# Narrow key ranges in a dilated attention, and another order of the opening transfers, in an f32 kernel of four joined layers

## The reference

```python
DILATION_GROUPS = ((128, 1), (512, 4), (2048, 16))     # (window, dilation)
# 8 query heads, 2 key/value heads, head dimension 128, 512 tokens
# causal dilated window: query t sees keys t, t-d, t-2d, ..., t-window
for g, (window, dilation) in enumerate(DILATION_GROUPS):
    o, l = dilated_window_attention(q[:, :, g], k[:, :, g], v[:, :, g], window, dilation)
...
wts = softmax(stack(lses))                              # over the three groups
o = sum(wts[..., None] * stack(outs))
```

## Time and profile before

| | us |
|---|---|
| Median of 3 runs (lowest, highest) | 3950.6 (3949.82, 3952.23) |
| The profiled execution, its own time | 3940.59 |
| Its span | 3938.6 |
| PE busy | 3680.1 (93% of the span) |
| DVE busy | 2036.6 (52%) |
| ACT busy | 798.5 (20%) |
| POOL busy | 1004.8 (26%) |
| Mean granted PE clock | 0.971 |
| DMA | 295.50 MB, mean 75 GB/s |

### The profile page before, as it was taken

The page is one execution under the profiler, slowest core; times in us unless marked ns, Lnnn a source line. Parts: engine busy times, 40 slices in busy tenths (PEclk is TensorE's granted clock), DMA queues, the critical chain, the costliest instruction groups (busy, mean ns, idle before and its releaser), DMA issues. The chain is left out here.

```text
span 3938.6 us, 37971 instructions
## 1 busy us (share of the span) xinstructions
PE 3680.1 (93%) x14476; PEld 2535.4 (64%) x14476; DVE 2036.6 (52%) x3522; ACT 798.5 (20%) x1606; POOL 1004.8 (26%) x964
## 2 busy tenths in 40 slices
PE   5999987999999999997899999999999998889999
PEld 3577334555555546633688884688886544778887
DVE  5820567676675530147664465755534224765543
ACT  2101455110010110154311113211111111421110
POOL 0100540322323100052334430234430000034443
PEclk9999998999999999998999999999999998999999
DMA  5422100133331111210122222222222210012222
GB/s 222 149 81 72 33 26 19 64 104 120 109 121 59 70 52 55 71 49 29 33 74 87 86 86 73 75 75 86 87 95 80 71 54 32 1 44 89 92 86 86
DMA packets 52100, 295.50 MB, mean 75 GB/s; under 512 B 5424, under 2 KB 5552, under 8 KB 25552
## 3 DMA queue, kind: packets, MB, share of 16 engines
q1 hardware_dynamic: 37808, 244.32, 18.1%
q10 hardware_dynamic: 9504, 31.98, 2.4%
q0 software_dynamic: 4608, 16.78, 1.3%
HBM read 290.57 MB, written 2.49 MB: 74 GB/s over the span
## 5 line engine op out<-in xcount | busy, mean ns | idle before, releaser
L2179 POOL TENSOR_TENSOR scratch<-ring 128x512 f32<-128x512 f32 (+1 forms) x148 | 187.3, 1265 | 1950.9 <-PE psum L575 1200.7
L575 PE MATMUL psum<-big,scratch 128*128 128x256 f32 (+1 forms) x2240 | 605.6, 426 | 0.0
L550 PE MATMUL psum<-H,ring 128*128 128x512 f32 x1184 | 560.5, 608 | 23.8 <-ACT H L1144 11.5
L575 PEld LDWEIGHTS psum<-big,scratch 128*128 128x128 f32 x2240 | 425.6, 190 | 163.7
L575 PE MATMUL psum<-H,scratch 128*128 128x256 f32 (+1 forms) x1856 | 435.7, 389 | 4.5 <-ACT cb L1074 3.2
L575 PE MATMUL psum<-big,ring 128*128 128x256 f32 (+1 forms) x1520 | 403.9, 418 | 13.7 <-DVE big L1719 4.9
L575 PEld LDWEIGHTS psum<-H,scratch 128*128 128x128 f32 x1856 | 350.6, 190 | 74.7 <-ACT cb L1074 8.7
L575 PE MATMUL psum<-H,ring 128*128 128x256 f32 (+1 forms) x1408 | 375.1, 411 | 9.4 <-ACT H L1144 4.2
L550 PEld LDWEIGHTS psum<-H,ring 128*128 128x128 f32 x1184 | 229.5, 195 | 237.1 <-issue 222.8
L575 PEld LDWEIGHTS psum<-big,ring 128*128 128x128 f32 x1520 | 287.7, 190 | 115.9 <-DVE big L1719 6.5
L575 PEld LDWEIGHTS psum<-H,ring 128*128 128x128 f32 x1408 | 272.3, 194 | 84.5 <-issue 9.3
(11 more groups left out here) (307 smaller groups left out, 4775.8 us busy)
## 6 DMA issues: line engine op xcount, KB each, us to landing
ring<-in_wall SPq DMA_DIRECT2D x202, 1024.0 KB, 4.9
big<-in_wada SPq DMA_DIRECT2D x48, 512.0 KB, 3.5
big<-in_wada POOLq DMA_DIRECT2D x32, 512.0 KB, 3.9
H<-negd ACTq DMA_DIRECT2D x16, 768.0 KB, 5.1
big<-in_wada ACTq DMA_DIRECT2D x4, 2048.0 KB, 28.3
scratch<-in_rpb ACTq DMA_DIRECT2D x16, 448.0 KB, 3.7
X<-in_xin SPq DMA_DIRECT2D x1, 3072.0 KB, 14.3
out<-X SPq DMA_DIRECT2D x1, 2048.0 KB, 7.2
```

The lines of the kernel that those rows point to most:

```text
L550: mm = pe.matmul(bank(b), lhsT, rhs_x(k0 + k), start=first, stop=last)
L575: mm = pe.matmul(fast_bank(st, q, b), lhsT, rhs(k), start=start and k == 0, stop=k == kt - 1, skip_group_check=True)
L2179: pool.tensor_tensor(s1, a21, a22, ALU.add).then_inc(combo_own, 1)
```

## The change

In the dilated attention, the 128 queries of a unit are cut into four blocks a of 32 (tokens 128a to 128a+127). A block needs at most the 256 keys from 128*max(a-1, 0) on, and only those are now computed. Scores of group 0 become four products of 32 queries with 256 keys, each writing its 32 partitions of PSUM; the values of group 0 become eight products (two key tiles for each of four blocks) of 32 queries, which accumulate into 32 partitions each. Masks, scores, exponentials, transposes and copies have 512 columns in place of 768; the mask tensor has 1280 columns in place of 2304. The units, the lists of the engines and their waits stay.

In the opening, X is sent in four parts, each with a semaphore of its own, after the constants and after the first group of modulation weights has landed; the ring slots wait for the third group. ACT waits for `cb` before it issues the modulation weights, and its squares wait for the parts of X one by one. Names of the unused branches are removed.

```diff
-NMASK2 = DIL * SEQ + 2 * P
+NMASK2 = DIL * 2 * P + 2 * P
...
-        x_in = sem("x_in")
+        x_in = [sem(f"x_in{g}") for g in range(4)]
...
+        ATTN = [(h, p) for h in range(QH2) for p in range(DIL)]
+
+        def near(a):
+            return max(a - 1, 0)
...
             sp.dma_start(cb[:], cvec.to_broadcast([P, 2 * D])).then_inc(cb_in, 16)
-            sp.dma_start(X_[:], xin).then_inc(x_in, 16)
...
             sp.dma_start(pos_s[0:ROPE2, :], pos.to_broadcast([ROPE2, SEQ])).then_inc(consts_in, 16)
-            for g in range(2):
-                sp.wait_ge(first_in[g], 16)
+            sp.wait_ge(first_in[0], 16)
+            for g in range(4):
+                at = slice(2 * g * TOK, 2 * (g + 1) * TOK)
+                sp.dma_start(X_[:, at], xin[:, at]).then_inc(x_in[g], 16)
+            sp.wait_ge(first_in[2], 16)
...
-                        pe.matmul(psum[:, s:s + 512], Q2[:, h, q * P:(q + 1) * P], K2[:, kv, :], start=True, stop=True)
...
+                    for a in range(4):
+                        pe.matmul(psum[32 * a:32 * a + 32, s:s + 256], Q2[:, h, q * P + 32 * a:q * P + 32 * a + 32],
+                                  K2[:, kv, near(a) * P:near(a) * P + 256], start=True, stop=True)
...
-                    for c, _ in key_tiles(u):
-                        mm = pe.transpose(psum[:, 2048 + c:2048 + c + P], Ssb[u % 2][:, c:c + P], ident)
+                    for c in range(4):
+                        mm = pe.transpose(psum[:, 2048 + c * P:2048 + (c + 1) * P], Ssb[u % 2][:, c * P:(c + 1) * P], ident)
...
-                    for i, (c, vals) in enumerate(kt):
-                        mm = pe.matmul(bank(6 + u % 2, n), PTs[u % 2][:, c:c + P], vals,
-                                       start=(i == 0), stop=(i == len(kt) - 1))
+                    for half in range(2):
+                        for a in range(4):
+                            pe.matmul(psum[32 * a:32 * a + 32, b * 512:b * 512 + P],
+                                      PTs[u % 2][:, half * P + 32 * a:half * P + 32 * a + 32],
+                                      V2[:, 0, near(a) + half, kv:kv + P], start=half == 0, stop=False, skip_group_check=True)
+                    for g in (1, 2):
+                        mm = pe.matmul(bank(b, P), PTs[u % 2][:, (1 + g) * P:(2 + g) * P], V2[:, g, q, kv:kv + P],
+                                       start=False, stop=g == 2, skip_group_check=True)
...
             def squares():
-                act.wait_ge(x_in, 16)
                 for k in range(DT):
+                    act.wait_ge(x_in[k // 2], 16)
                     act.activation(H[:, k, :], X[:, k, :], ACT.Square).then_inc(sq_done, 1)
...
-                    act.activation(Ssb[c][:, a:768], Ssb[c][:, a:768], ACT.Exp, bias=small[:, 194 + c:195 + c],
+                    act.activation(Ssb[c][:, 0:512], Ssb[c][:, 0:512], ACT.Exp, bias=small[:, 194 + c:195 + c],
...
-                    act.activation(PTs[u % 2][:, a:768], psum[:, 2048 + a:2048 + 768], ACT.Copy).then_inc(aPTs, 1)
+                    act.activation(PTs[u % 2][:, 0:512], bank(4), ACT.Copy).then_inc(aPTs, 1)
...
+            act.wait_ge(cb_in, 16)
             for g in range(4):
                 act.dma_start(B_[:, g * 4 * D:(g + 1) * 4 * D].rearrange("p (t k) -> p t k", k=D),
                               wada[4 * g:4 * g + 4].rearrange("t p k -> p t k")).then_inc(first_in[g], 16)
-            act.wait_ge(cb_in, 16)
...
-                        own(dve.scalar_tensor_tensor(x[:, 0:512], psum[:, s:s + 512], g, M2[:, q * 512:(q + 1) * 512],
-                                                     ALU.mult, ALU.add))
+                    own(dve.scalar_tensor_tensor(x[:, 0:256], psum[:, s:s + 256], g, M2[:, q * 256:(q + 1) * 256],
+                                                 ALU.mult, ALU.add))
...
-                    step(dve.tensor_reduce(small[:, 192 + c:193 + c], x[:, a:768], AX_X, ALU.max))
+                    step(dve.tensor_reduce(small[:, 192 + c:193 + c], x[:, 0:512], AX_X, ALU.max))
```

More of the change, by code:

```diff
@@ L778, in mlstm, with dilated_attention @@
                 turn(NH - 1)
-            def attention(which):
-                units = attn_units(which)
-                u0 = sum(UNITS[:which])
+            def dilated_attention():
                 def scores(u):
-                    h, q = units[u]
-                    s = (u % 2) * 1024
+                    h, q = ATTN[u]
+                    kv, s = h // (QH2 // KVH2), (u % 2) * 512
                     if u >= 2:
[L788 to L796, removed]
-                        pe.matmul(psum[:, s:s + 512], Q2[:, h, q * P:(q + 1) * P], K2[:, kv, :], start=True, stop=True)
-                        for g in (1, 2):
-                            mm = pe.matmul(psum[:, s + 384 + g * P:s + 512 + g * P], Q2[:, g * 8 + h, q * P:(q + 1) * P],
-                                           K2[:, 2 * g + kv, q * P:(q + 1) * P], start=True, stop=True)
-                    mm.then_inc(aS, 1)
[L803 to L811, removed]
@@ L830, in values @@
                     mm.then_inc(aO, 1)
                 scores(0)
-                for u in range(len(units)):
-                    if u + 1 < len(units):
+                for u in range(len(ATTN)):
+                    if u + 1 < len(ATTN):
                         scores(u + 1)
@@ L838, in attention @@
                         values(u - 1)
-                values(len(units) - 1)
+                values(len(ATTN) - 1)
             def na_attention(l):
@@ L1021, in _ @@
                 pe.wait_ge(acc_free[p], w.unit // 2)
-            attention(2)
-            pe.wait_ge(aY, sum(UNITS))
+            dilated_attention()
+            pe.wait_ge(aY, len(ATTN))
             turn_y([lambda t, i=i: Y2[:, t - CT, i * P:(i + 1) * P] for i in range(DT)], False)
@@ L1931, in na_attention, with dilated_attention @@
                         between[u]()
[L1933 to L1936, removed]
+            def dilated_attention():
                 def scores(u):
[L1940 to L1945, removed]
+                    h, q = ATTN[u]
+                    s, c = (u % 2) * 512, u % 2
+                    dve.wait_ge(aS, u + 1)
@@ L1946, in scores @@
                     if u >= 2:
-                        dve.wait_ge(aPT, u0 + u - 1)
+                        dve.wait_ge(aPT, u - 1)
                     x = Ssb[c]
[L1949 to L1955, removed]
-                        own(dve.scalar_tensor_tensor(x[:, 0:512], psum[:, s:s + 512], g, M2[:, q * 512:(q + 1) * 512],
-                                                     ALU.mult, ALU.add))
[L1958 to L1965, removed]
@@ new lines, in scores @@
+                    g = small[:, 344 + h * 4 + q:345 + h * 4 + q]
+                    own(dve.scalar_tensor_tensor(x[:, 0:256], psum[:, s:s + 256], g, M2[:, q * 256:(q + 1) * 256],
+                                                 ALU.mult, ALU.add))
+                    for i in (1, 2):
+                        a = 344 + (i * 8 + h) * 4 + q
+                        c0 = 128 + i * P
+                        ins = dve.scalar_tensor_tensor(x[:, c0:c0 + P], psum[:, s + c0:s + c0 + P], small[:, a:a + 1],
+                                                       M2[:, 1024 + (i - 1) * P:1024 + i * P], ALU.mult, ALU.add)
+                        if i == 1:
+                            own(ins)
@@ L1976, in finish @@
                 def finish(u):
-                    h, q = units[u]
+                    h, q = ATTN[u]
                     c = u % 2
-                    dve.wait_ge(aP, u0 + u + 1)
+                    dve.wait_ge(aP, u + 1)
                     r = small[:, 500 + c:501 + c]
                     step(dve.reciprocal(r, small[:, 496 + u % 4:497 + u % 4]))
[L1982 to L1986, removed]
+                    dve.wait_ge(aO, u + 1)
+                    dve.tensor_scalar(Y2[:, q, h * P:(h + 1) * P], bank(6 + c, P), r, None, ALU.mult).then_inc(aY, 1)
+                for u in range(len(ATTN)):
                     scores(u)
@@ L1989, in attention @@
                         finish(u - 2)
-                for u in (len(units) - 2, len(units) - 1):
+                for u in (len(ATTN) - 2, len(ATTN) - 1):
                     finish(u)
@@ L2233, in _ @@
             mix_weights(SW0)
-            pool.wait_ge(aO, sum(UNITS))
+            pool.wait_ge(aO, len(ATTN))
             mix_weights(YB)
@@ L2279, in _constants @@
     j = np.arange(P)[:, None]
-    s = np.arange(SEQ)[None]
+    key = P * np.maximum(j // 32 - 1, 0) + np.arange(2 * P)[None]
     for q in range(DIL):
-        dist = DIL * j + q - s
-        mask[:, q * SEQ:(q + 1) * SEQ] = np.where((dist >= 0) & (dist <= P), 0.0, NEG)
+        dist = DIL * j + q - key
+        mask[:, q * 2 * P:(q + 1) * 2 * P] = np.where((dist >= 0) & (dist <= P), 0.0, NEG)
     dist = j - np.arange(P)[None]
-    mask[:, 2048:2176] = np.where(dist >= 0, 0.0, NEG)
-    mask[:, 2176:2304] = np.where((dist >= 0) & (dist % 4 == 0), 0.0, NEG)
```

(2 more changed lines are left out.)

46 lines of the change are left out of this document (20 added, 26 removed).

## The result

The changed kernel takes 3914.3 us (median of 3 runs, 3910.5 to 3916.3) against 3950.6: ratio 0.9906, 95% interval 0.9883 to 0.9928, so 28 to 46 us less. In a second measurement (4 runs, beside 12 of the kernel before at 3948.9) it took 3917.1: ratio 0.9917 [0.9904, 0.9931], 32 us less. Forecast was 3918, with 32.2 less.

The account below looks back on a forecast made before the run. A closed chain over two units was taken to bound the dilated attention, TensorE close behind, and VectorE's gapless chain the opening. Attention 23.5 + opening 8.7 = 32.2 us less: 3950.6 - 32.2 = 3918, range 3907 to 3936.

Parts of the forecast that it names:

- The narrow passes overlap four ways: Dilated attention: narrow products in four column groups run together, 0.43 us for scores, 0.44 for values; forecast's own case, chance 0.52.
- The rival of pairs: Dilated attention: narrow passes overlap only two ways, TensorE 3.68 us per unit, 9 + 8.7 us less, 3933; chance 0.17.
- that of dispatch: Dilated attention: short passes start 0.07 us apart, 16 value passes take 1.1, 3.6 per unit, 3931; chance 0.12.
- in series: Dilated attention: narrow passes run one after another, 1.72 us for scores, 1.76 for values, kernel slower at 3988; chance 0.07.
- The price of changing shape: TensorE in dilated attention: going to narrow form costs 0.11 us, coming back 0.19, each twice per unit.
- The chain: Dilated attention: closed chain through TensorE, VectorE and ScalarE over two units goes from 7.93 to 6.45 us.
- the mis-sized term: Dilated attention: the cost of going narrow and back, put at 0.11 + 0.19 us in both scores and values.
- The stage: Dilated attention as a whole: 32 units, each 0.74 us shorter, 23.5 us less.
- The bound: Dilated attention: the chain, 3.23 us per unit, still bounds after the change; TensorE alone needs 2.8.
- The opening: Before the first projection: VectorE's gapless chain starts 8.7 us earlier, and all of it reaches the first projection.
- The 41: Opening: time in us by which the fourth weight group lands, needed at the reciprocal, forecast at 50.2.
- The cover of the squares: Opening: squares' one-column products end near 40, before the reciprocal at 50.2 needs them; cover everywhere 9 us or more.

## Why the prediction was right

- **The narrow passes overlap four ways.** Right, and shown for the scores: 8 passes of 256 columns and the next form 0.57 later; 1.84 when they share a column group. The earlier trace rows showed two groups side by side and could not tell of four; four was a choice with 0.52 behind it, and it came out as taken. The rival of pairs (3.68 per unit) falls on the 0.57, that of dispatch (16 short passes taking 1.1) on the 0.65 of L811. Where no change of shape follows them (3365.30 to 3365.77), the sixteen passes take 0.47, against 0.44 forecast and 1.76 in series. Together with the scores' passes and their way back to full width (0.54, 3363.24 to 3363.78) that is 1.01. The Trainium skill's 2.38 times for three column tiles ("TensorE: Matmul & The Clock Gate", Part 3) had given an estimated 1.1 for the passes alone, without any change of shape; the trace does not bear that out for four tiles.
- **The price of changing shape.** 0.30 a round trip was predicted from the earlier trace rows, 0.34 was measured by taking one away. Two round trips account for PE's 2.87 per unit against the predicted 2.8. This is in line with the Trainium skill, "TensorEngine Tiling (Array Packing)", Key Properties, by which a change of tiling mode drains TensorE.
- **The chain.** 6.54 for two units against 6.45. VectorE 2.00 (1.99), exponential 0.72 (0.71), copy 0.72 (0.74). Scores, transposes and values together are 3.10 (3.01): 1.32, 0.56 and 1.22 against 1.37, 0.46 and 1.18, where a start to start counts the way into narrow form with the row before it. The 0.09 are the mis-sized term, two round trips of shape at 0.04 more each.
- **The stage.** It gained 21.6, not 23.5. 1.3 of the difference are the mis-sized term: 32 units of half of (7.93 - 6.54) are 22.2. The starts from the fifth scores to the last gained 19.0 us in 27 units, 0.70 each, and the end, from the last scores to the last scaling, 1.6. The first four units gained only 0.9 (14.40 instead of 15.30), where four steady ones would gain 2.8. Meanwhile the clock was at its lower level, for 11.7 us of the stage instead of 4.8; that this is what they lack is argued, not tested. The prediction did not look there: its granted clock of 1.00 is from a stretch that began at 3333.00.
- **The bound.** A round trip less gained half of its 0.34 for each unit, and the copy's wait taken away shortened two units by 6.19 - 5.75 = 0.44. A chain over two units with PE close behind it says so; with PE as the bound the first would have gained all of the 0.34 and the second nothing.
- **The opening.** 8.7 predicted, 8.46 in the trace, up to 9.3 in the other executions of this order, 9.9 [5.1 to 13.4 by the interval] in the timed runs. Fourth issue at 11.59 (11.4 predicted), first projection 62.73 (62.5), `cb` at 5.23 (5.2), weights 12 to 16 in by 39.8 (41), squares' sums by 44 (40; X's four parts came one by one until 32.4). The 41 is wrongly added: its own terms, 12.0 MB from 7 at 0.4 MB/us, make 37. The cover of the squares was 6.5, not "9 us or more". A wrong part of the reasoning did no harm: I gave the early exponential to the wait for `cb`, which is worth nothing, and let the constants follow from it, where the move of X alone makes both.
- **The level.** The forecast for the profiled execution was 3908, it took 3914.3. Of the 6.3 us, 3.2 lie in the stretch of equal code shown above and 1.9 in the attention stage. The profiled execution of before was a short one (3940.6, its median 3950.6); the difference of medians was the right one to forecast. That 3918 met the second median (3917.1) so closely is partly luck: the attention gave some 2 us less than forecast and the opening, in most executions, a little more.

## What to carry to other kernels

Where an attention needs only a band of keys, cut the queries to 32 and give each block a column group of its own: here the passes of four such groups overlapped nearly in full. Count a round trip of shapes at about 0.34 us, as here, and order the products so that narrow ones follow on narrow ones. Then read the stage's chain again, since the buffers that the smaller tiles leave free (here a PSUM bank) may take the next wait away, which made this stage 8 us shorter. In an opening, find the first thing that the longest chain needs and look what is queued ahead of it: one large transfer in front of small constants held up both queues.

## What the runs showed of the hardware that was not expected

- X as one transfer of 24 KB rows, issued at 14.0, was in by 27.2; as four of 6 KB rows, issued from 14.8, by 32.4, beside the same 8 MB of weights. Whether the size of the rows or the number of transfers does it was not tried.
- How long an issue blocks depends on what other queues move: the fourth 2 MB issue ended at 17.4, at 10.7 to 11.6 or at 10.2 in three orders of the same transfers, when its queue had moved 1.2 to 1.5 MB.
- Four f32 products in four column groups, eight passes of 256 columns, take a third of the time that they take in one: 0.64 us against 1.91.
- The same instructions took 3220 to 3229 us in single executions, with the mean clock at 0.971 to 0.966.
- The attention stage begins at half clock, and with four narrow products side by side its full clock came 11.7 us after the first product, in seven executions; with the old products, or the four in one column group, after 4.8 to 4.9, in three.
